# One layer of a hybrid encoder on one core: raw rows first, moved bias split, and a shorter list of last parts

## The chip, the core and the metric

The kernel runs on one core of one Trainium2 chip, as a single program. TensorE (PE in the profile) does the matmuls and the transposes, VectorE (DVE), ScalarE (ACT) and GpSimd (POOL) do the rest, and sync (SP) issues most of the transfers. The metric is the device time of one execution in microseconds. The kernel before took 1539.73 us, the median of three runs from 1537.47 to 1541.36.

## The reference

One inference step of one layer for two groups of tokens that share all weights: 256 prompt tokens, and 8 samples of 16 tokens each with 512 cached positions. Together they are 384 rows of 1024 numbers, all float32. Cut to what matters:

```python
h = rmsnorm(x, g_mix)                                  # x * rsqrt(mean(x*x)+eps) * g
z = h @ w_in        # split: fox q, k, v (512 each), forget logits (8), q latent, kv latent (256), rotary key, two gates (1024)
fox_o  = softmax(q k^T * scale + forgetting, causal) @ v            # 8 heads of 64
mla    = softmax(q_lat ckv^T + q_rope krope^T, chunk-causal) @ ckv  # 8 heads
x = x + (sigmoid(g_a) * (fox_o @ w_o_fox) + sigmoid(g_b) * (mla_o @ w_o_mla)) @ w_out
x = x + cross_attend(rmsnorm(x, g_x), memory keys, memory values)   # 4 heads of 128, 256 memory rows
h = rmsnorm(x, g_ffn)
logits = h @ w_router + b_router; top 4 of 32 experts, softmax of their logits as weights
for each expert e and its rows:                        # w_gu[e]: 1024x2048, w_down[e]: 1024x1024
    gate, up = h @ w_gu[e] + b_gu[e], both clipped
    y += weight * (((up + 1) * gate * sigmoid(1.702 * gate)) @ w_down[e] + b_down[e])
out = rmsnorm(x + y, g_final)
```

The fox keys and values, forget logits, latents, rotary keys and the prompt's memory keys and values are outputs too.

## The kernel before

The 384 rows are three tiles of 128: two of the prompt, one of the samples. Every engine has one list of instructions written out by hand; engines wait for each other by semaphores. A PSUM result is a "group": `open_bank` gives the groups the eight banks in turn, `done` (or `give`, on the reader's side) counts a bank full (or free). Almost every matmul is issued by the helper `mm`, so its line is L520 in the profile; transposes have their own lines. A float32 matmul appears as two records.

**The start.** Sync loads three tiles of x, then the weights through a ring of eight slots, in the order of the list `stream`; a slot is loaded again when the last group that read it is full. ScalarE sums the squares of each tile (L1961), VectorE takes the inverse root by Newton steps in 13 small instructions (`inverse_root`, from L1469) and scales the rows in place (L1495). TensorE turns them (`rms_turn`, L534), VectorE copies the turned rows out and multiplies by the gain (`scale_turned`, L1501) into `hT`. Then come the projections: queries (`project_T`, the result turned), keys, forget logits and rotary key (`fl`), latents. ScalarE loads the constants (915 KB) right after the squares, ahead of nine smaller loads.

**The prompt's attention** (`doubles`, L830 to L840) runs 16 units of two heads in eight double rounds, each with scores, maximum (VectorE), exponential (ScalarE), division (VectorE), turning (TensorE, L790), copy (ScalarE), values (TensorE). Between them lie projections of the fox values and the turning of the first sample's cached keys (L665) and latents (L676). In round 8, the last but one, TensorE turns keys 2 and 3 and units 14 and 15 and takes the values of 12 and 13; in round 9 it turns the latents and takes the values of 14 and 15.

**The samples' attention** follows, sample by sample, then the gates (128 weight columns at a time), the two output projections of the attentions, the memory's key projection, `w_out`, the memory's value projection in two halves of columns, and the query projection. GpSimd loads the memory rows when the samples are done, writes the memory keys and values out, and then splits the experts' biases into three bf16 parts, 1024 columns at a time (L1396 to L1414, nine loads and moves and 15 computing instructions).

**The cross attention** has a part for the prompt, four units in a pipeline (L842 to L852: scores, turning two rounds later, values three rounds later), and one for the eight samples, a loop in which each round has the scores of sample b, the probabilities of b-1, the turning of the keys of b+1, one quarter of the output projection (`cross_out`), and the values of b-1. Then come the router's logits, the choice of four, and the table of the experts' order, which VectorE writes (`table_ready`, L1850).

**The experts.** Blocks of up to 64 rows run expert by expert, one block for most experts. Weights come in six tiles of 2 MB per expert, into eight homes. The first expert in order is always expert 0, so its six tiles are asked for early; for the second, sync waits for `table_ready` (L1314). A block's result is spread back over the rows as a matmul with a 0/1 matrix `share`, in bf16: the result is split into a high part (`yb[0]`, by ScalarE), a rest (`yrest`, by VectorE), a middle part `yb[1]` (ScalarE) and a low part `yb[2]` (VectorE), and all three are multiplied. This runs one block late, beside the next block's matmuls.

**The tail.** After the last block the same spreading stands alone: 18 bf16 matmuls into six banks, six additions to x (L1925), squares (L1961), the inverse root (L1469 on), GpSimd's product of each x tile with the final gain (L1424), a scaling by the root (L1932 on VectorE for tiles 0 and 2, L2276 on ScalarE for tile 1), and the output transfers.

## Time and profile before

| what | us |
|---|---|
| median of 3 runs | 1539.73 |
| the profiled execution, its own time | 1539.02 |
| its span (first to last instruction) | 1537.2 |
| TensorE busy | 1463.4 (95%) |
| VectorE busy | 554.5 (36%) |
| ScalarE busy | 313.5 (20%) |
| GpSimd busy | 50.4 (3%) |
| transferred | 483.48 MB |

A busy TensorE is not one at its peak, since its records overlap and their ends are modelled. The chain of waits says at each moment which engine or transfer the end depended on. A bracket behind a row of the timeline, as [1.84 <-DVE L1613], is the idle time of that engine before the row and what ended it. The granted clock is 1.00 at 2.4 GHz and 0.50 at 1.2 GHz.

### The profile page before, as it was taken

What the parts mean: (1) busy time and instruction counts of PE and PEld (TensorE: products, weight loads), DVE (VectorE), ACT (ScalarE), POOL (GpSimd) and SP (SyncE); (2) the same over time, 40 slices, a digit from 0 to 9 for tenths busy, and PEclk for the clock granted to TensorE, in tenths of its full rate; (3) what the DMA queues carried; (4) which work ended last, traced back from release to release, by engine and by line L of the source; (5) the groups of instructions that cost most, each with busy time, mean ns of one, the idle gap of its engine ahead of it and who ended that gap; (6) DMA issues with size and microseconds to landing.
All of it is one profiled execution on the core that took longest, in us unless ns stands there. A gap on an engine that the chain in (4) does not pass through costs nothing.

```text
span 1537.2 us, 21842 instructions
## 1 busy us (share of the span) xinstructions
PE 1463.4 (95%) x8240; PEld 718.2 (47%) x8241; DVE 554.5 (36%) x1231; ACT 313.5 (20%) x676; POOL 50.4 (3%) x56
## 2 busy tenths in 40 slices
PE   6998899999999898999999999999999999999994
PEld 4866677655688553333333333333333333333331
DVE  2245544100302456334343343343333433334234
ACT  1215555310001342111111111111111111111111
POOL 0000000000001600000000000000000000000001
PEclk9999999999999998999999999999999999999998
DMA  9411456832333259999999999999999999999993
GB/s 269 130 54 71 116 168 228 289 137 95 110 123 127 99 217 368 428 427 428 428 429 429 428 428 428 430 429 389 430 429 429 427 428 428 429 429 428 428 428 164
DMA packets 83037, 483.48 MB, mean 315 GB/s; under 512 B 18144, under 2 KB 46080, under 8 KB 56368
## 3 DMA queue, kind: packets, MB, share of 16 engines
q1 hardware_dynamic: 68800, 471.78, 75.1%
q0 software_dynamic: 3168, 9.11, 2.5%
q10 hardware_dynamic: 11024, 1.96, 0.7%
q8 instruction: 31, 0.51, 0.1%
q14 instruction: 14, 0.11, 0.0%
HBM read 475.16 MB, written 4.65 MB: 312 GB/s over the span
## 4 chain that ended last, share of the span: by engine, by line
PE 80%; DMA 14%; DVE 4%; issue 1%; ACT 1%; SPq 0%; ACTq 0%; DVEq 0%
PE bank L520 74%; DMA ring<-in_w_gu 13%; PE bank L1244 1%; PE bank L1169 1%; PE bank L665 1%; PE bank L534 0%; DVE small L1602 0%; PE bank L897 0%; DMA xr<-in_x_sample 0%; PE bank L676 0%; PE bank L790 0%; PE bank L1042 0%; DVE ring L1613 0%; DVE small L1603 0%; PE bank L938 0%
## 5 line engine op out<-in xcount | busy, mean ns | idle before, releaser
L520 PE MATMUL bank<-ring,hT 128*64 128x512 f32 (+3 forms) x3744 | 836.0, 562 | 14.1 <-DMA ring<-in_w_gu 12.9
L520 PEld LDWEIGHTS bank<-ring,hT 128*64 128x64 f32 (+1 forms) x3744 | 324.6, 146 | 440.7 <-issue 389.2
L1881 DVE SCALAR_TENSOR_TENSOR xr<-bank,probTs,xr 128x512 f32<-128x512 f32 x198 | 139.2, 745 | 231.1 <-PE bank L520 231.1
L520 PE MATMUL bank<-hT,ring 128*128 128x384 f32 x384 | 124.5, 486 | 1.3 <-DVE hT L1501 1.3
L2261 ACT ACTIVATE probTs<-hT 128x512 f32<-128x512 f32 x33 | 20.8, 631 | 440.7 <-DVE hT L1900 440.7
L1918 DVE TENSOR_TENSOR mlaT<-bank,foxT 128x512 f32<-128x512 f32 x33 | 22.8, 692 | 224.6 <-ACT foxT L2267 224.6
L520 PEld LDWEIGHTS bank<-hT,ring 128*128 128x128 f32 x384 | 72.7, 190 | 51.8 <-issue 1.7
L520 PE MATMUL bank<-foxT 64*128 64x512 bf16 x612 | 83.5, 379 | 3.0 <-DVE foxT L1921 3.0
L520 PE MATMUL bank<-ring 128*128 128x256 f32 (+6 forms) x332 | 62.6, 400 | 3.4 <-issue 3.4
L2267 ACT CAST foxT<-bank 128x512 bf16<-128x512 f32 x33 | 19.3, 586 | 215.7 <-PE bank L520 215.7
L520 PEld LDWEIGHTS bank<-foxT 64*128 64x128 bf16 x612 | 21.8, 94 | 83.5 <-issue 71.0
L1876 DVE SCALAR_TENSOR_TENSOR mlaT<-probTs,con 128x192 bf16<-128x192 f32 x66 | 27.4, 415 | 65.6 <-issue 65.6
L520 PEld LDWEIGHTS bank<-ring 128*128 128x128 f32 (+3 forms) x332 | 40.2, 164 | 16.8 <-issue 12.4
L1507 DVE COPY ring<-bank 128x512 f32<-128x512 f32 (+1 forms) x37 | 21.4, 595 | 66.5 <-PE bank L520 50.8
L2261 ACT ACT_TABLE_LOAD x33 | 42.3, 1283 | 0.6
L1956 ACT COPY ring<-bank 128x512 f32<-128x512 f32 (+2 forms) x44 | 21.5, 510 | 89.3 <-PE bank L520 86.6
L1424 POOL TENSOR_TENSOR ring<-xr,con 128x1024 f32<-128x1024 f32 x3 | 7.0, 2354 | 984.9 <-DVE xr L1925 984.9
L1900 DVE TENSOR_SCALAR hT<-bank 128x512 f32<-128x512 f32 x33 | 22.8, 692 | 44.9 <-PE bank L520 44.9
L2263 ACT COPY hT<-bank 128x512 f32<-128x512 f32 x33 | 19.3, 586 | 94.5 <-PE bank L1244 94.5
L520 PE MATMUL bank<-fqT,mlaT 128*64 128x512 bf16 x198 | 38.2, 379 | 0.0
L520 PE MATMUL bank<-att,foxT 96*64 96x512 bf16 x198 | 33.3, 385 | 2.8 <-issue 2.8
L520 PE MATMUL bank<-probTs,ring 128*128 128x128 f32 (+1 forms) x256 | 29.7, 287 | 1.0 <-ACT probTs L2106 0.8
(326 smaller groups left out, 1264.8 us busy)
## 6 DMA issues: line engine op xcount, KB each, us to landing
ring<-in_w_gu SPq DMA_DIRECT2D x128, 2048.0 KB, 23.7
ring<-in_w_down SPq DMA_DIRECT2D x64, 2048.0 KB, 25.9
ring<-in_w_in SPq DMA_DIRECT2D x16, 1024.0 KB, 11.0
ring<-in_cache_fox_k SPq DMA_DIRECT2D x8, 1024.0 KB, 4.8
ring<-in_cache_fox_v SPq DMA_DIRECT2D x8, 1024.0 KB, 7.7
ring<-in_cache_mla_ckv SPq DMA_DIRECT2D x8, 512.0 KB, 5.6
ring<-in_w_out SPq DMA_DIRECT2D x4, 1024.0 KB, 5.1
ring<-in_cache_mem_k SPq DMA_DIRECT2D x8, 512.0 KB, 3.3
```

The lines of the kernel that those rows point to most:

```text
L520: return pe.matmul(o, l, r, start=start, stop=stop, skip_group_check=True)
L665: i = pe.transpose(ps[:, P * k:P * k + P], k3[:, k, P * g:P * g + P], ident)
L1169: i = pe.transpose(turned[:, P * k:P * k + P], x, ident)
L1507: give(v.tensor_copy(dst, ps[:, 0:n] if n else ps), key)
L1876: return v.scalar_tensor_tensor(dst, bc(gslot[:, :, e], [P, NT, CAP]), cc("i64")[:, b], iota1, ALU.subtract, ALU.is_equal)
L1881: v.scalar_tensor_tensor(x, sums[i % 2][:, :], gate_e[:, i // 2, e], x, ALU.mult, ALU.add).then_inc(shares_added, 1)
L1900: v.tensor_scalar(gS, gate[:, :], LIMIT, None, ALU.min).then_inc(gate_clipped, 1)
L1918: v.tensor_tensor(yrest, yp[:, :], yb[0], ALU.subtract).then_inc(y_rest, 1)
L1956: give(a.copy(dst, ps[0:rows, 0:n] if n else ps), key)
L2261: a.activation(sS, gS, ACT.Sigmoid, scale=ALPHA).then_inc(gate_sig, 1)
L2263: a.copy(actT, aTp[:, :].rearrange("p (k t) -> p k t", t=CAP)).then_inc(actT_ready, 1)
L2267: a.copy(yb[0], yp[:, :]).then_inc(y_high, 1)
```

## The change

It edits five places and leaves the rest as it is.

1. **Start.** TensorE turns the raw rows as soon as they have landed. VectorE multiplies by the gain only, into a new buffer `rawT`. The first projections are the fox keys (their weights are now first in the stream), from `rawT`; VectorE scales each key row by its inverse root as it copies the result out. The root of tiles 0 and 1 is taken after two square sums, that of tile 2 afterwards. For the other projections a small matmul of all ones with the diagonal matrices of the roots spreads the 384 roots over all partitions (`roots`), and VectorE writes `hT = rawT * roots` in two halves. ScalarE loads the constants after the nine smaller loads.
2. **The prompt's attention, round 8.** Values of units 12 and 13 and the latents are put ahead of the turning of units 14 and 15, on TensorE and on ScalarE.
3. **Bias split.** GpSimd does it right after it has asked for the memory rows, ahead of writing the memory keys and values out. `bmid` gets another place, and ScalarE's wait for `bias_moved` stands ahead of the cross attention.
4. **Cross attention.** One projection, of the second half of the memory values of tile 1, moves into round 1 of the prompt's units; the first sample's scores move into round 5, and the turning of the third sample's keys moves behind the scores of the second. Waits for the values' copies are put where they are needed.
5. **Tail.** TensorE multiplies the high part while VectorE takes the rest, and then the rest itself in float32, with a float32 copy of `share` that GpSimd makes (`share32`). Middle and low part are not used after the last block. GpSimd multiplies only tile 1 by the final gain; for tiles 0 and 2 VectorE does gain and root in one instruction.

```diff
+        rawT = qlf[:, 0:3072].rearrange("p (k t) -> p k t", k=KD)
...
-        bmid = low[0:NE, 5120:5632].bitcast(BF16)
+        bmid = fkf[0:NE, 0:512].bitcast(BF16)
...
-            rms_turn("hT", lambda t: (xn_ready, t + 1), range(NT))
...
+            rms_turn("hT", lambda t: (x_loaded[t], 16), range(NT))
+            for j in range(2):
+                arrived(pe, ("fk", j))
+                for t in range(NT):
+                    if j == 0:
+                        for half in range(2):
+                            pe.wait_ge(free(("hT", t, half)), count(("hT", t, half)))
+                    i = project(("fk", t, j), ("fk", j), t, rawT)
+                used_last(pe, i, ("fk", j))
+                if j == 0:
+                    pe.wait_ge(ones_ready, 1)
+                    pe.wait_ge(diag_of_roots, 1)
+                    ps = open_bank(pe, "roots")
+                    for t in range(NT):
+                        i = mm(ps[:, P * t:P * t + P], all_one, root_diag[:, t, :], t == 0, t == NT - 1)
+                    done(i, "roots")
...
                     between_doubles(i)
+                    last = i == NU // 2
+                    if last:
+                        double_values(2 * i - 4)
+                        turn_latents(0)
                     if 1 <= i <= NU // 2:
                         for u in (2 * i - 2, 2 * i - 1):
                             turn(u, UNITS[u])
-                    if i >= 2:
+                    if i >= 2 and not last:
                         double_values(2 * i - 4)
...
-            mem_project("xv", (1,))
+            mem_project("xv", (1,), (0,))
...
+            def between_units(i):
+                if i == 1:
+                    mem_turn(1)
+                    mem_project("xv", (1,), (1,))
+                if i == 5:
+                    mem_scores(0)
+
+            pipeline(XUNITS, U_MEM, between_units)
...
-            pe.wait_ge(y_split, nblk + 1)
             pe.wait_ge(shares_added, nblk * 6 + 1)
...
+            for pair, banks in enumerate(pairs):
+                for half, o in enumerate(halves_of):
+                    mm(banks[half][:, :], share[o, P * pair:P * pair + P], yb[0][o, :], True, False)
+            pe.wait_ge(share_wide, 1)
+            pe.wait_ge(y_rest, nblk + 1)
+            for pair, banks in enumerate(pairs):
+                for half, o in enumerate(halves_of):
+                    mm(banks[half][:, :], share32[o, P * pair:P * pair + P], yrest[o, :], False, True).then_inc(shares_full, 1)
...
-            rms_rows(0, NT, xr, xr)
+            v.memset(all_one, 1.0).then_inc(ones_ready, 1)
+            dve.wait_ge(square_sum, 2)
+            inverse_root(rstd[:, 0:2], ssq[:, 0:2], D)
             dve.wait_ge(g_mix_loaded, 16)
             for t in range(NT):
-                scale_turned("hT", t, gm_c, hT)
+                scale_turned("hT", t, gm_c, rawT)
+            dve.wait_ge(square_sum, NT)
+            inverse_root_of_one(rstd[:, 2:3], ssq[:, 2:3], D)
...
+            for half in range(2):
+                k = slice(4 * half, 4 * half + 4)
+                last = v.tensor_tensor(hT[:, k, :], rawT[:, k, :], bc(ps[:, 0:TOK].unsqueeze(1), [P, 4, TOK]), ALU.mult)
+                last.then_inc(h_ready, 1)
...
+                last = i == NU // 2
+                if last:
+                    for u in (2 * i - 4, 2 * i - 3):
+                        values_out(u, UNITS[u])
                     latents_out(0)
...
-            for t in range(NT):
-                pool.wait_ge(shares_added, nblk * 6 + (2 * t + 3))
-                nc.gpsimd.tensor_tensor(weighed[:, t, :], xr[:, t, :], gfin, ALU.mult).then_inc(x_weighed, 1)
+            pool.wait_ge(share_ready, nblk + 1)
+            nc.gpsimd.tensor_tensor(share32, share, share, ALU.mult).then_inc(share_wide, 1)
+            pool.wait_ge(shares_added, nblk * 6 + 5)
+            nc.gpsimd.tensor_tensor(weighed[:, 1, :], xr[:, 1, :], gfin, ALU.mult).then_inc(x_weighed, 1)
...
-                v.tensor_scalar(yout[:, t, :], weighed[:, t, :], rstd[:, n0 + t:n0 + t + 1], None, ALU.mult).then_inc(fin_ready[t], 1)
+                v.scalar_tensor_tensor(yout[:, t, :], xr[:, t, :], rstd[:, n0 + t:n0 + t + 1], gfin, ALU.mult, ALU.mult).then_inc(fin_ready[t], 1)
```

## Rows read from the trace of the kernel before

**Rows 1.** Page, throughput in 40 equal slices of the span.

```profile
GB/s 269 130 54 71 116 168 228 289 137 95 110 123 127 99 217 368 428 427 428 428 429 429 428 428 428 430 429 389 430 429 429 427 428 428 429 429 428 428 428 164
```

**Rows 2.** Page, chain that ended last, shares of the span by engine.

```profile
PE 80%; DMA 14%; DVE 4%; issue 1%; ACT 1%; SPq 0%; ACTq 0%; DVEq 0%
```

**Rows 3.** Windows: engines' busy us, then granted clock, transfer share, GB/s.

```profile
590.00:595.00 5.00, 2.14 (x12) 1.15 (x12) 4.23 (x17) 1.63 (x2) 0.00 (x0) 0.80 0.30 75
```

**Rows 4.** Timeline of the start: start us, duration us, engine, line, operation, count.

```profile
2.10 24.79 SPq L1292 DMA_DIRECT2D ring<-in_w_in  x8
...
7.11 0.19 ACT L1961 ACTIVATION_READ_ACCUMULATOR probTs<-xr 128x1 f32 x1
...
9.48 0.17 DVE L1469 TENSOR_SCALAR rstd<-small 128x3 f32<-128x3 f32 x1 [9.37 <-ACT probTs L1961]
...
12.06 2.08 DVE L1495 TENSOR_SCALAR xr<-xr,rstd 128x1024 f32<-128x1024 f32 x3
...
12.96 4.37 PE L534 MATMUL bank<-con,xr 128*128 128x128 f32 x24 [12.96 <-DVE xr L1495]
...
15.79 2.59 DVE L1501 TENSOR_TENSOR hT<-bank,small 128x512 f32<-128x512 f32 x4 [0.16 <-PE bank L534]
...
18.63 20.88 PE L520 MATMUL bank<-hT,ring 128*128 128x384 f32 x64 [1.30 <-DVE hT L1501]
```

**Rows 5.** Transfers asked for at 2.1 and at 1.2 us: KB, us to landing.

```profile
ring<-in_w_in SPq DMA_DIRECT2D x1, 1024.0 KB, 10.4
...
small<-in_g_mix ACTq DMA_DIRECT2D x1, 4.0 KB, 8.4
```

**Rows 6.** Timeline of the prompt attention's last two rounds.

```profile
177.01 1.04 PE L790 MATMUL bank<-con,ring 128*128 128x128 f32 x8
...
177.79 1.09 ACT L1956 COPY probTs<-bank 128x512 f32<-128x512 f32 x2
...
179.10 0.76 ACT L2039 COPY foxT<-bank 64x256 f32<-64x256 f32 x2 [0.22 <-PE bank L520]
...
180.14 1.09 PE L520 MATMUL bank<-probTs,ring 128*64 128x128 f32 x16
...
180.62 1.06 ACT L2066 COPY ring<-bank 32x128 f32<-32x128 f32 x4
```

**Rows 7.** Windows of the pause and the stretch behind it.

```profile
170.00:172.00 2.00, 0.00 (x0) 0.00 (x0) 1.93 (x6) 1.51 (x7) 0.00 (x0) 1.00 0.47 66
...
174.00:176.00 2.00, 2.00 (x14) 1.34 (x13) 1.05 (x3) 1.02 (x3) 0.00 (x0) 0.50 0.30 41
```

**Rows 8.** Windows of the cross attention; the first busy time is TensorE's.

```profile
500.00:520.00 20.00, 16.60 (x71) 10.96 (x69) 8.61 (x14) 6.86 (x19) 14.51 (x12) 1.00 0.35 121
520.00:540.00 20.00, 15.89 (x146) 11.33 (x146) 9.60 (x23) 8.73 (x27) 10.27 (x12) 1.00 0.24 79
```

**Rows 9.** Timeline of the cross attention.

```profile
516.65 0.66 PE L790 MATMUL bank<-con,ring 128*128 128x128 f32 x4 [1.84 <-DVE ring L1613]
...
530.57 2.20 DVE L1727 TENSOR_SCALAR ring<-ring,small 128x256 f32<-128x256 f32 x1
...
534.09 3.60 PE L520 MATMUL bank<-ring,fkT 128*128 128x512 f32 x8
```

**Rows 10.** Timeline of the tail.

```profile
1516.67 0.69 DVE L1918 TENSOR_TENSOR mlaT<-bank,foxT 128x512 f32<-128x512 f32 x1 [6.79 <-ACT foxT L2267]
...
1518.98 2.12 PE L520 MATMUL bank<-foxT 64*128 64x512 bf16 x18 [2.97 <-DVE foxT L1921]
1519.94 4.04 DVE L1925 SCALAR_TENSOR_TENSOR xr<-bank,probTs,xr 128x512 f32<-128x512 f32 x6 [1.20 <-PE bank L520]
...
1521.44 6.96 POOL L1424 TENSOR_TENSOR ring<-xr,con 128x1024 f32<-128x1024 f32 x3 [984.88 <-DVE xr L1925]
...
1526.16 2.26 DVE L1470 TENSOR_SCALAR rstd<-rstd 128x3 int32<-128x3 int32 x1
...
1530.75 1.42 DVE L1932 TENSOR_SCALAR ring<-ring,rstd 128x1024 f32<-128x1024 f32 x2
```

More of the change, by code:

```diff
@@ L404, in build @@
         for j in range(2):
+            tile(("fk", j), whole(KD, 256, w_in[:, :, C_FK + 256 * j:C_FK + 256 * j + 256]))
+        for j in range(2):
             tile(("fq", j), whole(KD, 256, w_in[:, :, C_FQ + 256 * j:C_FQ + 256 * j + 256]))
-        for j in range(2):
-            tile(("fk", j), whole(KD, 256, w_in[:, :, C_FK + 256 * j:C_FK + 256 * j + 256]))
         tile("fl", [(lambda s: kview(s, KD, 40)[:, :, 0:8], w_in[:, :, C_FL:C_FL + 8]),
@@ L463, in home @@
             return (NTILE * turn + c) % NHOME
+        share32 = big[:, HOME_AT[0]:HOME_AT[0] + TOK]
         def expert_tile(turn, c):
@@ L554, in _ @@
             pe.wait_ge(ident_loaded, 16)
-            rms_turn("hT", lambda t: (xn_ready, t + 1), range(NT))
-            for t in range(NT):
-                for half in range(2):
-                    pe.wait_ge(free(("hT", t, half)), count(("hT", t, half)))
+            rms_turn("hT", lambda t: (x_loaded[t], 16), range(NT))
+            for j in range(2):
+                arrived(pe, ("fk", j))
[12 more added lines that the diff above has]
+                    done(i, "roots")
             for j in range(2):
@@ L798, in values @@
                 pe.wait_ge(free(("T", u)), count(("T", u)))
+                if hs[0] == 2:
+                    for m in range(2):
+                        pe.wait_ge(free(("xv", m, 1)), count(("xv", m, 1)))
                 ps = open_bank(pe, ("V", u))
@@ L995, in _, with mem_project @@
                             used_last(pe, i, (w, j))
-            def mem_project(w, halves=range(2)):
+            def mem_project(w, halves=range(2), tiles=range(2)):
                 for j in halves:
                     arrived(pe, (w, j))
-                    for t in range(2):
+                    for t in tiles:
                         i = project((w, t, j), (w, j), t, memT)
-                    used_last(pe, i, (w, j))
+                    if t == 1:
+                        used_last(pe, i, (w, j))
             for t in range(2):
@@ L1270, in _ @@
             pe.wait_ge(share_ready, nblk + 1)
-            pe.wait_ge(y_split, nblk + 1)
             pe.wait_ge(shares_added, nblk * 6 + 1)
-            for pair, banks in enumerate((sums, (gate, up), (turned, aTp))):
-                for n, part in enumerate(yb):
-                    for half in range(2):
-                        o = slice(CAP * half, CAP * half + CAP)
-                        i = mm(banks[half][:, :], share[o, P * pair:P * pair + P], part[o, :], n == 0, n == 2)
-                        if n == 2:
-                            i.then_inc(shares_full, 1)
+            pe.wait_ge(y_high, nblk)
+            pairs = (sums, (gate, up), (turned, aTp))
+            halves_of = [slice(CAP * half, CAP * half + CAP) for half in range(2)]
+            for pair, banks in enumerate(pairs):
[6 more added lines that the diff above has]
+                    mm(banks[half][:, :], share32[o, P * pair:P * pair + P], yrest[o, :], False, True).then_inc(shares_full, 1)
         @block.sync
@@ L1414, in _ @@
                 pool.wait_ge(bias_moved, 32 * c + 32)
+            for w, m, o in (("xk", mk, "p_mem_k"), ("xv", mv, "p_mem_v")):
+                pool.wait_ge(free((w, 1, 1)), count((w, 1, 1)))
+                pool.dma_start(out[o].rearrange("l b (t p) h n -> p (l b t) (h n)", p=P), m).then_inc(mk_written, 16)
             nc.gpsimd.tensor_copy(before, con[:, t0:t0 + P]).then_inc(sums_ready, 1)
@@ L1965, in _ @@
                 squares(t, xr[:, t, :])
-            load(con[:, P:NCONST], d["constants"][:, P:NCONST])
             load(gx_c, turned(d["g_x"][0], KD), slow=True)
@@ L1976, in _ @@
             load(wr[:, :, :], d["w_router"][0].rearrange("(k p) e -> p k e", p=P))
+            load(con[:, P:NCONST], d["constants"][:, P:NCONST])
             for k in range(KT):
@@ L2085, in _ @@
                         probs_out(u, UNITS[u])
-                if i >= 2:
+                if i >= 2 and not last:
                     for u in (2 * i - 4, 2 * i - 3):
@@ L2152, in _, with mem_rows_out @@
                         squares(NT + t, memx[:, t, :])
-            def mem_rows_out(w, m):
-                for j in range(2):
-                    for t in range(2):
-                        copy_out((w, t, j), m[:, t, 256 * j:256 * j + 256], 256)
+            def mem_rows_out(w, m, parts=((0, 0), (1, 0), (0, 1), (1, 1))):
+                for t, j in parts:
+                    copy_out((w, t, j), m[:, t, 256 * j:256 * j + 256], 256)
             mem_rows_out("xk", mk)
```

80 lines of the change are left out of this document (47 added, 33 removed).

## The prediction, made before the change was run

> **What bounds the kernel now.** I read first the throughput line of the page: from the slice that begins at 576 us on, the transfers move about 428 GB/s almost without a break [rows 1]. Next the chain of waits by engine: 80% TensorE, 14% transfers, all other engines 6% [rows 2]. So there are two regimes. Until about 590 us TensorE works nearly without a break, and an engine's wait counts only where it leaves TensorE idle. From then on the experts' weights arrive as one stream: 192 tiles of 2 MB are 403 MB, and at 428 GB/s that is 941 us of the 1537. The reader is to see in the 5 us window at 590 what ties the regimes together: transfers are busy at 0.30 only [rows 3]. The six tiles of the first expert have landed, and the next may not be asked for before the expert table exists (sync waits for `table_ready`). From there to the end stands a fixed quantity of transfer. Hence the rule for everything below: time taken off ahead of the table comes off the end one for one; time taken off inside the expert loop is worth nothing; time behind the last tile counts again. That leaves four places that the change touches: the start, the end of the prompt's attention, the cross attention, and the tail.
>
> **1. The start: raw rows, key projections first.** Now: the third square sum releases the root at 9.48, the scaling of the rows starts at 12.06, the transposes run from 12.96 to 17.3, VectorE copies them out, and the first projection starts at 18.63 [rows 4]. After: the transposes need only the rows of x and end near 9.5. The root of two tiles starts when the second square sum is there (7.11 + 0.19 = 7.3) and takes what the root takes now, 12.06 - 9.48 = 2.6, so to 9.9; the two copies of tile 0 take 0.65 each (2.59 for four) and end at 11.2. The gain vector, 8.4 us after its request at about 1.2, is there by then. The first weight tile is not: asked for at 2.10, landing 10.4 later, at 12.5 [rows 4, 5]. I take 12.5 as the new start of the projections, 6.1 us earlier. The remaining scaling (3.4 us of it for hT, 1.2 for the root of tile 2, copies of the keys) lies beside twice 10.3 us of key projection (a projection is 16 records of 256 columns, each two thirds of the 0.326 us of a 384-column one [rows 4]: 3.5 us; three of them per half), since the queries come only after the second half. The roots' spread costs 3 float32 matmuls of 128 columns, together the two records of one 384-column matmul: 2 x 0.326 = 0.65 us [rows 4]. The constants' big load is queued behind nine others now; nobody reads it before the forget logits, after 50 us.
> The clock: the 24 transposes take 0.18 us each though they follow one another, while eight at 177.01 take 0.13 [rows 4, 6]: TensorE starts slowly, and now the transposes pay for it. After the change they are over three microseconds before the projections start, so the projections pay again. 24 x (0.18 - 0.13) = 1.3 us is the price I take; after the pause at 170 us the granted clock is 0.50 [rows 7], and 7 us at that would cost 3.5. Sum: 6.1 - 0.65 - 1.3 = **4.2 us**; ends 2.0 (cost 3.5) and 5.5 (no cost).
> The Trainium skill, "TensorE: Matmul & The Clock Gate", section "What's actually happening", says that the default state is the throttled one and that activity releases it. This trace agrees in the durations (0.18 against 0.13 us), not in the granted clock, which reads full there. [...]
>
> **2. The end of the prompt's attention.** Now in the last but one round TensorE runs: keys, turning of units 14 and 15 (177.01 to 178.05), values of 12 and 13, latents, then at 180.14 the values of 14 and 15, without a pause [rows 6]. After: values of 12 and 13 and the latents go ahead of the turning. ScalarE follows that order: values out 0.76, one latent copy 0.55, four small copies 1.06, and only then the two probability copies, 1.09 for both [rows 6]. Values of 12/13 (1.09, as at 180.14) would end at 178.1, so ScalarE's queue ends at 178.2 + 0.76 + 0.55 + 1.06 + 1.09 = 181.7, and the values of 14 and 15 start there instead of at 180.14. The long pause nearby, with TensorE idle from 170 to 172 [rows 7], belongs to the round before, whose order stays. **Loss 1.6 us**; ends: a gain of 0.5 if the units' probabilities would have been late, a loss of 2.5 if the clock falls in the new pause.
>
> **3. The cross attention.** The windows from 500 to 540 show TensorE busy 16.60 + 15.89 of 40 us: 7.5 us idle [rows 8]. Two causes. Dependency: four units are too few to fill the way TensorE, VectorE, ScalarE, VectorE and back (1.84 us before the first turning [rows 9]). And GpSimd: while its bias split runs, VectorE's instructions between memory and memory wait for its own: 2.20 us for a scaling of 128x256 [rows 9], where one of 128x1024 takes 0.71 at the end of the kernel (1.42 for two [rows 10]). The change moves the split to about 294 to 340 us, beside the gates, where VectorE has next to nothing to do and the next wait for its rows is at 394; its new waiters (ScalarE before the cross attention) come 170 us later, so it costs nothing there. It also moves 16 records of value projection (3.6 us) from ahead of this stage into its second round, ahead of the first turning, and the first sample's scores into the fifth. Neither adds work. Idle then: the turning of unit 0 comes 3.6 us later than its predecessor's wait of 1.84, so that wait goes; the others shrink by the port waits of 1 to 2 us. What is late next is the second sample's probabilities, a chain of about 2 us with one transpose and one set of values in front of it; I leave 1.5 us. **Gain 6.0 us**; ends 3.5 (4 us of idle stay) and 7.5 (none). The keys' and values' write-out now ends some 60 us ahead of the sync queue's wait for it, and the ring slot of the moved projection is asked for again at about 514, one tile that is read at 528.
>
> **4. The tail.** Now: rest at 1516.67 (0.69), middle part on ScalarE, low part on VectorE, 18 bf16 matmuls from 1518.98, the six additions from 1519.94 for 4.04; squares; a root whose second instruction, on three numbers per partition, takes 2.26 while GpSimd multiplies three tiles (6.96 from 1521.44); two scalings from 1530.75, 1.42 [rows 10]. The squares follow the last addition by 1.2, so this root ran from 1525.2 to 1530.7, 5.5 against the 2.6 of the first. After: the high parts run while the rest is taken; the first float32 pair starts at 1517.4 and takes two records of 0.43 us, 0.86 (3.60 for eight of 128x512 [rows 9]), if its two halves run side by side as the bf16 ones do. Additions from 1518.4, of 0.67 each, end at 1522.5 instead of 1524.0. GpSimd has one tile, from the fourth addition (1521.2) for 2.3, to 1523.5; the root starts at 1523.7, is free of it, and takes 2.6: 1526.3. Two products, at most twice the 0.67 of an addition of half the width, end at 1528.9 instead of 1532.2. **Gain 3.3 us**; ends 2.0 (halves one after the other, or a collision) and 4.5.
> The Trainium skill, "GPSIMD Engine Reference", section "Specifications", says that the memory interfaces are shared with VectorE's instructions in a two-port mode or with two memory inputs. It speaks against this step: the scaling is replaced by a product with two memory inputs. The trace agrees as far as it goes (2.26 us for that tiny instruction); by that rule a late GpSimd would hold the first product by up to 2.3 us, and the tail would give about 1.
>
> **Sum.** 4.2 - 1.6 + 6.0 + 3.3 = 11.9 us. The profiled execution took 1539.02 (span 1537.2), 0.7 less than the median of 1539.73. 1539.0 - 11.9 = 1527.1; with the median's 0.7 I forecast **1527.8**.
>
> **The rivals.**
> - *The start gives nothing* (tile later, clock low through the whole first projection): 11.9 - 4.2 = 7.7, so 1532.0. For it: the slow transposes, and a tile that lands only just in time. Against it: the 64 records from 18.63 average 0.326 us, full speed nearly from the first [rows 4]. Chance 0.14.
> - *The gain ahead of the table is capped*: if the first six tiles don't move up with it, only the transfer pause of about 3.5 us at 590 can be saved [rows 3], and 3.5 + 3.3 = 6.8 gives 1532.9. Against it: the same rounds that make the table release these tiles. Chance 0.08.
> - *More*: no loss in step 2 and all idle of step 3 gone, 11.9 + 1.6 + 1.5 = 15.0, 1524.7. Chance 0.12.
> - *Slower*: the new pause in step 2 lies 3 us behind a stretch at half clock [rows 7], directly ahead of the samples' attention, 110 us of short matmuls with pauses. If TensorE stays at 1.2 GHz there, each us of it costs 0.5. From 24 us on the gain is used up; half the stage (55 us) gives 1539.7 - 11.9 + 27 = 1555. Against it: the records at 180.14 (0.07 us each) are at full speed again, behind the longer pause at 170 [rows 6]. Chance 0.04.
> - *Nothing changes* (the moved work was hidden, the forecast terms cancel): 1539.7. Chance 0.03.
>
> **How the numbers follow.** The forecast has 0.59. The ends of the four terms add up to 2.0 - 2.5 + 3.5 + 2.0 = 5.0 and to 5.5 + 0.5 + 7.5 + 4.5 = 18.0; all at one end is unlikely. The range goes from 1522.0 to 1535.0: it holds the first three rivals and leaves out the slower one, the unchanged one and the outermost sums. A change below 0.3% (4.6 us), about what a measurement of this kernel can't tell from none, is a time over 1535.1. Faster: 0.59 + 0.12 nearly whole, most of 0.14 and of 0.08, 0.88. Same: the rest of these and the last case, 0.07. Slower: 0.05.
>
> **What would show it.** First projection record at 12 to 13 us and no TensorE pause between the two key halves and the queries. Idle before the values of units 14 and 15. The windows of the cross attention with 1 to 2 us idle, no VectorE instruction of that stage over its usual length, GpSimd busy between 294 and 340. The request behind the expert table about 8.6 us earlier than 593.2, and the loop's length unchanged. A root of 2.6 us at the end. The forecast is wrong if the first request behind the table moves less than 6 us, or if the low clock spreads.

## The result and the profile after

The changed kernel takes 1525.64 us (median of 4 runs, 1524.85 to 1526.94), the kernel before in the same session 1540.55: ratio 0.9903, 95% interval 0.9889 to 0.9917. It is 14.9 us faster; 11.9 were forecast (1527.8 against 1525.64). A second set on another chip (e9 below) gave 0.9901 (0.9886 to 0.9916). The profiled execution took 1525.61, its span 1523.7, 13.5 less than before's 1537.2.

The throughput line still shows one stream, now from the slice that begins at 571 us, with its small dip in the 28th slice as before (386 GB/s, 389 before) [rows 1], and the chain of waits by engine is nearly as before [rows 2]:

```profile
GB/s 286 131 67 46 116 184 214 306 153 87 111 125 83 152 262 360 428 427 428 429 428 428 428 429 428 428 428 386 429 429 428 429 428 428 428 429 428 428 428 197
```

```profile
PE 79%; DMA 16%; DVE 2%; issue 1%; ACT 1%; SPq 0%; DVEq 0%; ACTq 0%
```

The start [rows 4]: the 24 transposes run as soon as the rows have landed and take longer than before, 5.47 us; the first projection waits for its weight tile, not for VectorE, and starts at 11.58, 7.05 us earlier than at 18.63. The queries follow the keys at 33.05 without a pause.

```profile
2.11 12.58 SPq L1329 DMA_DIRECT2D ring<-in_w_in  x5
...
4.64 5.47 PE L543 MATMUL bank<-con,xr 128*128 128x128 f32 x24 [4.64 <-DMA con<-in_constants]
...
11.58 21.63 PE L529 MATMUL bank<-ring 128*128 128x256 f32 x102 [1.47 <-DMA ring<-in_w_in]
```

The end of the prompt's attention [rows 6]: ScalarE's small copies (four, 1.06) now stand ahead of the two probability copies, and TensorE waits 1.79 us for them. From the first turning of that round to the values of the last two units the trace of before has 7.40 us (172.74 to 180.14), this one 9.39 (166.38 to 175.77).

```profile
172.94 1.04 PE L806 MATMUL bank<-con,ring 128*128 128x128 f32 x8
...
173.51 1.06 ACT L2123 COPY ring<-bank 32x128 f32<-32x128 f32 x4
174.59 1.07 ACT L2013 COPY probTs<-bank 128x512 f32<-128x512 f32 x2
...
175.77 1.09 PE L529 MATMUL bank<-probTs,ring 128*64 128x128 f32 x16 [1.79 <-ACT probTs L2013]
```

The windows of the cross attention [rows 8]: TensorE is busy 18.95 and 19.37 of 20 us, and GpSimd is all but out of it (1.28 us).

```profile
500.00:520.00 20.00, 18.95 (x126) 15.25 (x125) 9.88 (x26) 10.95 (x32) 1.28 (x3) 1.00 0.44 162
520.00:540.00 20.00, 19.37 (x161) 10.77 (x160) 8.52 (x22) 7.11 (x23) 0.00 (x0) 1.00 0.35 129
```

I measure this stage from the first of the 64 records of the query projection to the first output projection, and count the 3.62 us of value projection where it lies ahead: before 489.15 to 534.09 [rows 9], 44.94 + 3.62 = 48.56; after 42.19. The gain is 6.37. The request behind the expert table goes out at 582.42 instead of 593.16, 10.7 us earlier, where 8.6 were forecast. The transfer pause is still there, 10 us earlier [rows 3]:

```profile
580.00:585.00 5.00, 2.64 (x13) 1.59 (x14) 4.35 (x16) 1.63 (x2) 0.00 (x0) 0.84 0.36 80
```

The tail [rows 10]: the additions run from 1508.79, GpSimd takes one product, none of the root's steps is slow, and the two last products take 1.24 each.

```profile
1506.71 0.69 DVE L1977 TENSOR_TENSOR mlaT<-bank,foxT 128x512 f32<-128x512 f32 x1 [6.79 <-ACT foxT L2335]
1506.82 0.82 PE L529 MATMUL bank<-foxT 64*128 64x512 bf16 x6 [0.78 <-ACT foxT L2335]
...
1507.54 2.85 PE L529 MATMUL bank<-mlaT,ring 64*128 64x512 f32 x12
...
1508.79 4.04 DVE L1982 SCALAR_TENSOR_TENSOR xr<-bank,probTs,xr 128x512 f32<-128x512 f32 x6 [1.39 <-PE bank L529]
...
1511.59 2.35 POOL L1461 TENSOR_TENSOR ring<-xr,con 128x1024 f32<-128x1024 f32 x1 [11.12 <-DVE xr L1982]
...
1514.25 0.17 DVE L1507 TENSOR_SCALAR rstd<-rstd 128x3 int32<-128x3 int32 x1
...
1516.76 2.48 DVE L1989 SCALAR_TENSOR_TENSOR ring<-xr,rstd,con 128x1024 f32<-128x1024 f32 x2 [0.16 <-DVE rstd L1513]
```

From the cast of the last high part to the last output's request it is 16.36 us before (1516.05 to 1532.41) and 13.18 after (1506.09 to 1519.27): 3.2 gained.

### The profile page after: what moved, and what is told of

The parts are those of the page before. It is cut to its first block, busy times and chain, and to the rows that moved or that the text cites. A ratio compares the mean times of both kernels' runs of the same rounds, so it can differ in the third digit from the quotient of the medians.

```text
span 1523.7 us, 21869 instructions
## 1 busy us (share of the span) xinstructions
PE 1466.4 (96%) x8246; PEld 719.8 (47%) x8247; DVE 552.8 (36%) x1240; ACT 313.2 (21%) x676; POOL 45.4 (3%) x55
## 4 chain that ended last, share of the span: by engine, by line
PE 79%; DMA 16%; DVE 2%; issue 1%; ACT 1%; SPq 0%; DVEq 0%; ACTq 0%
PE bank L529 73%; DMA ring<-in_w_gu 16%; PE bank L1278 1%; PE bank L683 1%; PE bank L1203 1%; DMA ring<-in_w_in 1%; PE bank L920 0%; PE bank L806 0%; PE bank L694 0%; PE bank L1066 0%; DVE small L1661 0%; PE bank L543 0%; DVE ring L1672 0%; PE bank L961 0%; DVE xr L1982 0%
## 5 line engine op out<-in xcount | busy, mean ns | idle before, releaser
L529 PE MATMUL bank<-ring,hT 128*64 128x512 f32 (+3 forms) x3648 | 813.9, 566 | 15.4 <-DMA ring<-in_w_gu 14.6
L529 PEld LDWEIGHTS bank<-ring,hT 128*64 128x64 f32 (+1 forms) x3648 | 305.6, 145 | 439.3 <-issue 387.2
L529 PE MATMUL bank<-ring 128*128 128x256 f32 (+7 forms) x434 | 84.6, 394 | 4.0 <-issue 2.5
L529 PEld LDWEIGHTS bank<-ring 128*128 128x128 f32 (+3 forms) x434 | 58.7, 170 | 20.2 <-issue 11.5
```

Of the source, the lines that this page charges most:

```text
L529: return pe.matmul(o, l, r, start=start, stop=stop, skip_group_check=True)
```

## The experiments

Each kernel is the changed one with the edit named. Time ratios have intervals of 0.13 to 0.15% on each side (2 us and more), so I read stage lengths in the profiles first and the times second.

**e1: the order of the prompt's last round put back.**

```
+                if i == 9:
+                    turn_latents(0)
...
-                    last = i == NU // 2
-                    if last:
-                        double_values(2 * i - 4)
-                        turn_latents(0)
```

> The changed kernel with its order in the last round of the prompt's attention put back (the first sample's latents turned in round 9, the products with the values behind the turns); all else as changed. Theory (the move keeps no gap filled and delays the first sample's scores): the first sample's scores come 2.0 us earlier against the round's start than in the changed kernel (13.8 us behind it instead of 15.8), all later marks keep that lead, and the time falls by 2.0 us, 1523.6. Rival 1 (the gap reappears elsewhere ahead of the expert blocks): the second sample's scores are as late as in the changed kernel and the time stays at 1525.6. Rival 2 (the move did gain and the trace of two executions misleads): the time rises by up to 0.5 us.

Measured: 1523.9 us (4 runs), ratio to before 0.9885 (0.9871 to 0.99). In its round the values of the last two units start 7.55 us behind the first turning, not 9.39:

```profile
167.93 1.97 PE L808 MATMUL bank<-con,ring 128*128 128x128 f32 x8 [3.68 <-DVE ring L1670]
...
175.48 1.09 PE L529 MATMUL bank<-probTs,ring 128*64 128x128 f32 x16
```

This part of the change cost 1.84 us in the stage. The medians of the time differ by 1.7, but the intervals of the two ratios overlap, so the time alone doesn't show it. What I had not expected is the 167.93: it is 1.5 us later than in the changed kernel, though nothing ahead of it differs. See e9.

**e2: the whole start put back** (roots ahead of the transposes, query projections first, the constants' large load early).

```
-            rms_turn("hT", lambda t: (x_loaded[t], 16), range(NT))
+            rms_turn("hT", lambda t: (xn_ready, t + 1), range(NT))
```

> The changed kernel with the start as before: roots ahead of the transposes, scaled rows turned, query projections first, the large load of constants early. Theory (what is gained ahead of the expert blocks counts one to one): the latents' transposes come at 94.1 us instead of 87.8, the time is 6.4 us more, 1532.0. Rival 1 (my price of the low clock was right and something else gave the 2.2 us that came on top): a rise of 4.2 us, 1529.8. Rival 2 (the start is absorbed by a later wait on a transfer): under 1 us, below 1526.7.

Measured: 1531.17 (6 runs), 0.9934 (0.9922 to 0.9946), so 0.0031 or 4.8 us over the changed kernel's ratio. The latents' transposes come at 94.15 against 87.75, 6.4 later, and the first expert block at 590.30 against 583.78. The start reaches the end, by 5 to 6 us (4.8 by the ratios, 5.9 between the two profiled executions); the times leave open how much of the 6.4.

**e3: GpSimd's split of the biases back beside the cross attention.**

```
+            pool.wait_ge(free(("xk", 1, 1)), count(("xk", 1, 1)))
...
+            pool.wait_ge(free(("xv", 0, 1)), count(("xv", 0, 1)))
+            pool.wait_ge(mix_ready, KD)
             pool.wait_ge(ckv_written, 32)
             for c in range(3):
```

> The changed kernel with POOL's split of the biases back beside the cross attention of the prompt (it starts when three of the four value projections of the memory are out) instead of beside the samples' attention. Theory (POOL's work slows DVE's small operations, and each of the prompt's units waits for DVE): of the 6.4 us that the stage gained, 2.5 go again, 1528.1, and DVE's 128x3 and 128x256 operations of the stage are back at 1 to 2 us. Rival (the moved projection alone filled the waits): within 0.5 us of 1525.6, whatever DVE's durations do.

Measured: the stage 43.81 us, 1.6 longer; 1529.63 (5 runs), 0.9922 (0.9909 to 0.9935). The groups of VectorE instructions (line, operation, shapes, count, busy us, mean ns) from 500 to 520, of the changed kernel:

```profile
L1672 DVE TENSOR_TENSOR ring<-ring,small 128x512 f32<-128x512 f32 x4 | 2.8, 692 | 0.1
...
L1662 DVE TENSOR_SCALAR small<-small 128x2 f32<-128x2 f32 x4 | 0.7, 170 | 0.1
```

and of e3:

```profile
L1675 DVE TENSOR_TENSOR ring<-ring,small 128x512 f32<-128x512 f32 x4 | 5.3, 1336 | 0.1
...
L1665 DVE TENSOR_SCALAR small<-small 128x2 f32<-128x2 f32 x4 | 1.0, 254 | 0.1
```

One shape doubles in its mean, the other grows by half. The means hide that single instructions are hit: of the four 128x512 two keep 0.69 us, one takes 2.63 (it starts at 511.39, beside a GpSimd operation of 2.12 from 511.35) and one 1.33. So which instruction is slow depends on where GpSimd's operations fall, and my expectation named the wrong ones: the scalings of 128x256 stay at 0.35 to 0.50 here. The stage lost 1.6, not 2.5. The median of the time rose by 4.0, more than the stage; the profiled execution, at 1525.31 the shortest of the five, had no stretch at half clock behind the narrow projection (see e9), which hides the loss in it.

**e4: the second half of the value projection, tile 1, back ahead of the stage.**

```
-            mem_project("xv", (1,), (0,))
+            mem_project("xv", (1,))
```

> The changed kernel with the second half of the memory's value projection, tile 1, back ahead of the cross attention, all else as changed. Theory (PE's 3.6 us of it lie in waits of the first two units' steps): 3.5 us of the 6.4 go again, 1529.1, as idle PE in the first units. Rival (with the split gone the units no longer wait long enough to hold it): under 1.5 us, below 1527.1.

Measured: 40.36 + 3.62 = 43.98 us, 1.8 longer; 1527.86 (4 runs), 0.9915 (0.9901 to 0.993). So moving 3.62 us of work hid only 1.8 of it, between theory and rival. That the rest of the waits that it could fill had gone with the split is likely; no run has the split back and this projection moved back without the third edit.

**e5: the samples' first scores and exponentials back behind the stage.**

```
-                if i == 5:
-                    mem_scores(0)
...
-                if 0 < b < NB:
+                if b < NB:
                     mem_scores(b)
```

> The changed kernel with the first memory scores of the samples, their exponentials and the third turn of memory keys back behind the prompt's cross attention. In the changed kernel this stage (from the query projection's 64 records of 128x384 to the first output projection) takes 42.19 us, 6.37 less than before; with the split back it grew by 1.6, with the projection back by 1.8. Theory (the three fill separate waits): it grows by the missing 3.0 us here, to 45.2, and the time to 1528.6. Rival (the split and the projection cover one another's absence, so each alone shows too little): it grows by under 1 us, 1526.3.

Measured: the stage 43.22 us, 1.0 longer (484.56 to 527.78), where the theory had 3.0 and the rival under 1. The time, 1529.32 (6 runs, 1526.24 to 1532.54; 0.9921, 0.9909 to 0.9934), rose by more. In the profiled execution (1529.87) that is no effect of the edit: it came to this stage 3.2 us late with nothing edited ahead of it. By the latents' transposes it was 0.35 late (88.10); behind them its granted clock is at 0.50 from 116 to 124 and at 0.79 to 128, where the changed kernel's is full from 120. What the other five executions lost there isn't recorded.

**e10: e3, e4 and e5 together.**

> The changed kernel with all of its third part undone: split beside the cross attention, whole value projection ahead of it, the samples' first scores behind it. Alone they cost the stage 1.6, 1.8 and 1.0 us. Theory (they cover one another: one wait can hold only one of them, and POOL's split makes the waits longer): together 6.4, the whole gain of the stage, 1532.0. Rival (they add): 4.4, 1530.0, and the rest of the stage's gain has another cause.

Measured: 1533.41 (5 runs), 0.9944 (0.9929 to 0.9958). The stage: 486.18 to 532.15, 45.97 + 3.62 = 49.6, 7.4 longer than in the changed kernel and 1.0 longer than before. Singly the three cost 1.6 + 1.8 + 1.0 = 4.4. So they are not a sum, as the theory had it: with the split away, the waits are short and there is little to fill; with it there, the fillers have more to fill. Which of the three covers which is not separated. The extra 1.0 over the kernel before is luck of position and of the clock. Up to the first sample's turning the stage runs as before's, 2.97 us earlier; there GpSimd holds two scalings of 128x256, for 2.27 and 1.58 us where 0.35 is usual (before: one, 2.20), and TensorE waits for the first:

```profile
524.48 2.27 DVE L1780 TENSOR_SCALAR ring<-ring,small 128x256 f32<-128x256 f32 x1
...
526.80 0.69 PE L1081 MATMUL bank<-con,ring 128*128 128x128 f32 x2 [3.45 <-DVE ring L1780]
...
527.28 1.91 PE L1063 MATMUL bank<-con,ring 128*128 128x128 f32 x8
```

The last row is what follows that wait: the granted clock is 0.50 from 528 to 530, and the eight transposes take 1.91 us where the kernel before has 1.04, the sixteen records behind them 1.04 instead of 0.64. So up to 1.3 of the 7.4 is the clock; 6.1 or more are left, still well over 4.4.

**e6: the last products as before** (GpSimd weighs three tiles).

```
+            for t in range(NT):
+                pool.wait_ge(shares_added, nblk * 6 + (2 * t + 3))
+                nc.gpsimd.tensor_tensor(weighed[:, t, :], xr[:, t, :], gfin, ALU.mult).then_inc(x_weighed, 1)
```

> The changed kernel with the last products as before: POOL weighs three tiles, DVE and ACT only scale. Theory (POOL's 128x1024 products beside the root stretch DVE's 128x3 steps): the root takes 5.5 us instead of 2.6, the two scalings 1.4 instead of 2.5, the time rises by 1.8 us, to 1527.4; the additions keep their time, so 1.4 of the tail's 3.2 us belongs to the float32 rest. Rival (the root's steps were slow for another reason): the root stays at 2.6 us and the time falls by 1.0, to 1524.6.

Measured: the tail 15.16 us (1506.01 to 1521.17) against 13.18: 2.0 longer; 1529.21 (5 runs), 0.9922 (0.9909 to 0.9934). The slow step of the root is back, beside GpSimd's products:

```profile
1510.19 6.96 POOL L1462 TENSOR_TENSOR ring<-xr,con 128x1024 f32<-128x1024 f32 x3 [9.80 <-DVE xr L1983]
...
1514.92 2.26 DVE L1508 TENSOR_SCALAR rstd<-rstd 128x3 int32<-128x3 int32 x1
...
1519.51 1.41 DVE L1990 TENSOR_SCALAR ring<-ring,rstd 128x1024 f32<-128x1024 f32 x2
```

Of the 3.2 us of the tail 2.0 belong to the products and 1.2 to the float32 rest.

**e7: twelve more transposes per expert block on TensorE.**

```
+                for _ in range(3):
+                    for k in range(4):
+                        pe.transpose(turned[:, P * k:P * k + P], ident, ident)
                 turn_rows()
```

> The changed kernel with twelve more transposes of 128x128 on PE in every expert block, into a bank that is overwritten after (1.3 us per block, some 43 us in all over 33 blocks). Theory (the weights' stream sets the loop): from the first block to the end of the last it stays within 1 us of 923.0, the time within 1 us of 1525.6. Rival (PE, 96 percent busy on the page, sets it): 1568.

Measured: 1546.69 (5 runs), 1.0037 (1.0024 to 1.005). Neither theory holds. From the first block to the last shares the loop is 20.5 us longer (1506.82 to 1527.33, the first block starting at 583.78 in both within 0.2). Twelve transposes take 1.31 us, in 33 blocks 43.2: some 22.7 were hidden. The windows of the changed kernel and of e7:

```profile
600.00:1000.00 400.00, 393.35 (x2190) 142.52 (x2188) 149.69 (x247) 60.21 (x87) 0.00 (x0) 1.00 1.01 428
1000.00:1100.00 100.00, 98.40 (x540) 34.81 (x538) 34.37 (x57) 15.02 (x21) 0.00 (x0) 1.00 0.98 413
1100.00:1500.00 400.00, 393.64 (x2194) 142.81 (x2192) 151.09 (x249) 60.21 (x87) 0.35 (x1) 1.00 1.01 428
```

```profile
600.00:1000.00 400.00, 400.00 (x2302) 154.65 (x2300) 145.54 (x238) 58.58 (x84) 0.00 (x0) 1.00 1.01 428
1000.00:1100.00 100.00, 100.00 (x590) 39.76 (x586) 37.30 (x61) 14.84 (x22) 0.00 (x0) 1.00 0.88 370
```

The stream runs at 428 GB/s in both but for the window at 1000, where it waits for TensorE to free tiles: 43 GB/s less over 100 us are 4.3 MB, 10 us of stream. The other 10 are TensorE's lag behind the stream at the end: by windows of 5 us the transfers stop about 1509 us here and about 1499 in the changed kernel, and the last shares come 20.5 us later. By this sum, an estimate, TensorE has about 11 us to spare in each half of the loop, no more.

**e9: the changed kernel again.**

> The changed kernel itself once more, beside the other kernels of this chip: what two sets of runs of one kernel differ by. Theory (the same trace, with the stretches at half clock behind the start and behind the narrow projection differing from execution to execution): 1525.6 to 1528, and the profile's marks within 0.2 us of the first profile's except behind such a stretch. Rival (the differences between the kernels tried so far are all edits): 1525.6 within 0.5.

Measured: 1526.87 (4 runs, 1524.87 to 1527.21), 0.9901 (0.9886 to 0.9916). The stage of the cross attention is 42.19 again. The latents' transposes come at 89.39, not 87.75, 1.64 later. The reason stands in the windows of the first key projections, at 12 to 16 us, of the first profile and of this one:

```profile
12.00:14.00 2.00, 2.00 (x11) 1.77 (x10) 1.97 (x6) 0.00 (x0) 0.00 (x0) 1.00 1.23 302
14.00:16.00 2.00, 2.00 (x11) 1.74 (x11) 1.72 (x9) 0.00 (x0) 0.00 (x0) 1.00 1.25 292
```

```profile
12.00:14.00 2.00, 2.00 (x7) 1.59 (x7) 1.90 (x7) 0.00 (x0) 0.00 (x0) 0.57 1.24 299
14.00:16.00 2.00, 2.00 (x7) 1.62 (x6) 1.55 (x7) 0.00 (x0) 0.00 (x0) 0.58 1.25 292
```

The key projections up to the first query take 21.5 us where the clock is full (11.58 to 33.05). Of the 12 profiled executions with the new start, 7 take that, within 0.1, and 5 take longer with the same instructions: e1, e5, e9 and e11 by 1.5 to 1.7, e10 by 2.9. What TensorE did before is not the same in them, though. Between the last transpose and the first projection it stood idle for 1.00 to 1.78 us in the seven (e4, e6, the changed kernel's first profile, e12, e7, e8, e3) and for 1.81 to 2.75 in the five (e1, e9, e11, e5, e10), the longest pause with the largest loss. The row of this run:

```profile
11.49 23.34 PE L529 MATMUL bank<-ring 128*128 128x256 f32 x102 [1.89 <-DMA ring<-in_w_in]
```

The pause is what is left between the end of the transposes and the landing of the weight tile (in e7 VectorE's last copy), and from execution to execution the one moves by 1.1 us and the other by 0.7. That the length of the pause decides fits all twelve; no edit has set it, so as a cause it is not shown. A second such stretch follows the narrow projection (48 records of 40 columns, about 0.1 us each), with no pause ahead of it: the 144 records from there take 29.57 us in the changed kernel's profile and 26.24 in e3's, where the clock stayed full. Of the nine profiles with the new start that have the narrow projection ahead of the next one, five lost 3.3 us there, three (e4, e5, e10) 1.7, and only e3 nothing.

**e8: three edits to beat the change:** e1's order, the narrow projection interleaved with the next one, and the experts' table ahead of the last third of the row gather, with VectorE's memsets behind it.

```
+                for k in range(KD):
+                    i0 = mm(narrow[:, 0:40], hT[:, k, P * t:P * t + P], kview(slot("fl"), KD, 40)[:, k, 0:40], k == 0, k == KD - 1)
+                    i1 = mm(wide[:, 0:256], hT[:, k, P * t:P * t + P], kview(slot("kv"), KD, 256)[:, k, 0:256], k == 0, k == KD - 1)
...
+                if t == 2:
+                    pe.wait_ge(diag_ready, 8)
+                    mm(yp[:, 0:256], ones[0:NE, :], table, True, True).then_inc(table_full, 1)
```

> A kernel to beat the changed one, three edits that can be read apart in the profile: the order of the prompt's last round put back; the narrow projection (128x40) interleaved with the next one (128x256) step by step instead of ahead of it; the experts' table multiplied ahead of the last third of the row gather, with DVE's memsets moved behind the table's copies. Theory: the order gives 1.8 us; the table is copied 1.2 us earlier and so is all behind it; the stretch at half clock behind the narrow projection (3.3 us lost in the changed kernel's profile) goes, 2 us on average over executions; together 5.0, 1520.6. Rivals: the clock falls all the same, then 1522.6; the later gather delays the loop, which shows as a first block later than now with nothing gained from the table, 1523.8.

Measured: 1524.77 (4 runs), 0.9895 (0.9881 to 0.991), no better than e1. The last output projection starts at 553.81, 3.7 ahead of the changed kernel, but the last shares at 1504.63, 2.2 ahead. The interleaving did its part: full clock in every window from 52 to 76. The table did not: the wait for it ends earlier, but after the tile asked for behind it the sync queue waits for the sample tile's low part, 8.1 us instead of 5.1 (waits of the sync queue from 560 to 700: line, what was waited for, us in total, times, longest; the changed kernel first, then e8):

```profile
SPq L1358 <- DVE con L1829: 5.1, 1, 5.1
```

```profile
SPq L1360 <- DVE con L1831: 8.1, 1, 8.1
```

**e11: e8 without the table.**

> The changed kernel with the order of the prompt's last round put back and the narrow projection interleaved with the next, without the earlier table. Theory (the earlier table gained nothing since the row gather behind it made the first block late and the next tile waits for the sample tile's low part): the lead of e8 at the last output projection (3.7 us over the changed kernel) now reaches the end; 1.0 to 1.5 us below e8, 1523.5. Rival (what is gained ahead of the loop is lost in it whatever the table does): as e8, 1524.8.

Measured: 1522.54 (4 runs), 0.988 (0.9865 to 0.9895). From the last output projection to the last shares 949.36 us (554.82 to 1504.18), against 949.33 in the changed kernel and 950.82 in e8: the table alone cost 1.5. The ten profiles that have this part as in the changed kernel scatter there from 948.2 to 949.4 (e7's longer loop left out), so the 1.5 is clear of that scatter, though its size is not exact.

**e12: e8 and the sample tile's low part earlier.**

```
+            x_high_out(2)
             act.wait_ge(rows_full, 1)
...
+            high_part(2)
...
+            low_part(2)
```

> e8 with one more edit: the sample tile's high part is cast by ACT before the gathered rows are copied, and DVE takes its differences ahead of the gate weights, so its low part is ready 2 us earlier (the changed kernel's SyncE queue waits 5.1 us for it, e8's 8.1). Theory (the queue's two waits bind in turn: table, then low part): the transfer pause behind the first tile goes and the end is 2 us ahead of e8's, 1522.8. Rival (the first block's own release of the tiles binds by then): the dip in the transfers only moves, 1524.5.

Measured: 1520.66 (4 runs, 1519.83 to 1522.12), 0.9865 (0.985 to 0.988): the fastest kernel here, faster than both given ones. Against e8 the same stretch is 1.8 shorter (553.51 to 1502.55, 949.04), as the theory had it. Against e11 it is only 0.3, inside the scatter, so most of e12's 1.9 us over e11 is not shown to be an edit (e11's profile lost 1.5 in the start by the clock, e12's nothing), and the earlier table and low part together gain nothing that shows over the changed kernel: the lead is that of e11's two edits. The transfer pause did not go as the theory had it, nor did it move as the rival had it. At 576 it is as deep as in e8 (67 and 57 GB/s); the dip behind the next tile, at 584, is shallower (250 and 127), with the wait for the low part 6.0 us instead of 8.1. The granted clock is 0.50 from 572 to 584 in both.

```profile
576.00:580.00 4.00, 3.22 (x9) 1.02 (x8) 2.24 (x9) 0.58 (x1) 0.00 (x0) 0.50 0.35 67
580.00:584.00 4.00, 2.94 (x10) 1.30 (x12) 3.24 (x6) 2.19 (x2) 0.00 (x0) 0.50 0.98 406
584.00:588.00 4.00, 4.00 (x15) 1.27 (x13) 1.42 (x7) 0.14 (x1) 0.00 (x0) 0.65 0.80 250
```

## Why the prediction was right, and where its terms were off

- **Start, forecast 4.2, measured 6.4** (7.05 less 0.65 for the roots' spread; the latents' transposes lead by 6.36). Two terms were mis-sized. I took the weight tile at 12.5; it was there at 11.5, 1.0 earlier. It landed 9.4 us after its request instead of 10.4, and between 9.2 and 9.9 in all twelve executions with the new start; in e2, where the constants' 915 KB are asked for early again, it took 11.5. So the likely reason is a part of the change that I had counted at nothing, the large load moved behind the small ones; no run moves it alone. And I charged 1.3 for a slow clock behind the new pause; it was 1.47 us long in the profiled execution, where I had expected over 3, and nothing was lost behind it. e9 shows that the price is real and about what I took, 1.64, but paid only in some executions, the 5 of 12 with the longest pauses. Spread over these it is 0.8 (1.6 four times, 2.9 once, over 12), so a typical gain is about 5.6, between the forecast and the first profile; e2's ratio gives 4.8, and the intervals of the two ratios together leave nearly 3 on each side. That the first profile paid nothing was luck.
- **End of the prompt's attention, forecast -1.6, measured -2.0** (-1.84 by e1). The chain on ScalarE went as worked out: the values' copies, one latent copy (VectorE takes the other), four small ones, two probability copies, then the values on TensorE.
- **Cross attention, forecast 6.0, measured 6.37.** Both causes that I named are shown (GpSimd by e3, unfilled waits by e4 and e5), and that they are not a sum (e10: 7.4 together, 4.4 singly). My picture of the moved projection was too simple: of its 3.62 us only 1.8 pay in the changed kernel.
- **Tail, forecast 3.3, measured 3.2.** The root took 2.6 as forecast, the first shares' pairs ran side by side, the additions started 1.2 earlier relative to the last high part (1.5 forecast), and two products took 2.48 where I allowed 2.7. The rule of the Trainium skill, "GPSIMD Engine Reference", section "Specifications", that spoke against the products did not bind, since GpSimd was done at 1513.94 (1511.59 + 2.35), 0.1 us before the root began at 1514.04; that a late GpSimd would hold a product with two memory inputs agrees with e3's 1336 against 692 ns.
- **The rule for the loop** (nothing inside it counts) holds for this change and is too broad. The profile has the loop 0.8 longer (from the first block to the last high part's cast, 922.31 against 921.53). In e1, e2, e3, e4 and e9 the stretch from the first block to the last shares is 922.2 to 922.6, in the first profile 923.04: a scatter of 0.8 between executions, as large as what was to be explained. But e7 shows TensorE's slack as some 22 us over the loop, not without end; and e8 shows that the table's time does not count one for one by itself: the tile after the next waits for the low part, the one after that for TensorE.
- **The sum.** 6.4 - 2.0 + 6.37 + 3.2 is 14.0; the profile loses 0.8 in the loop, which is 13.2, and the rest to 13.5 lies behind the last request. So the forecast's 11.9 was 2.1 too small in the four terms, nearly all of it the start's. The medians differ by 14.9, 1.4 more than the profiled pair. That is within what executions of one kernel differ by: the four here spread over 2.1 us, the four of the kernel before over 5.0 (1537.47 to 1542.45).
- The cap by the transfer pause did not come: the pause moved up with the table (581 instead of 591), since the tiles ahead of it did. The slower rival did not come either: from 185 to 480 the granted clock is 1.00 in every window of 50 us.
- That the projections would pay again behind the pause was too strong: 7 of 12 paid nothing. The Trainium skill, "TensorE: Matmul & The Clock Gate", section "What's actually happening", says that the default is the throttled state and names idleness as what brings it back; it does not say that every pause does. The twelve starts agree with that much, since the five that fell had the longest pauses. The fall behind the narrow projection, with no pause ahead of it, idleness does not explain.

## What to carry to other kernels

When a background job and a latency chain share an engine's memory path, move the job first and measure the chain again before filling its waits: the two gains are not a sum. Ahead of a long transfer stream a gain counts only down to the next condition of the queue that feeds it, so list all of them (table, low part, freed tile), not the first. And before a forecast says that work in a stream-bound loop is free, work out how much of it is: here TensorE was 98% busy and free for 22 us of 923.

## What the runs showed of the hardware that I had not expected

- The same instructions have stretches at half clock in some executions and not in others: at the start of the key projections in 5 of 12 profiles (1.5 to 2.9 us lost, behind pauses of 1.81 to 2.75 us; none behind 1.00 to 1.78), behind the narrow projection from nothing (e3) to 3.3 us. In e3's five runs the one with mean clock 0.988 took 1525.31 and the two with 0.983 took 1529.79 and 1530.15.
- Narrow matmuls ahead of wide ones went with the low clock in ten of eleven profiles (the kernel before and e2 among them); mixed step by step with them they did not, in three kernels of three (e8, e11, e12: full clock in all windows from 52 to 76). That the mixing is the cause is likely, not proven, since e3 had full clock without it.
- VectorE beside GpSimd, float32 between memory and memory: 128x2 from 170 to 817 ns (mean of four, e10), 128x512 with two operands from 692 to 1336 (mean of four, e3; the longest 2630), 128x256 from 353 to 2270 and 1580 (e10); a maximum read from a bank stayed at 690 (685 in e10).
